# Adding the squared rows of two RMS norms on Pool, with one ones-matmul per tile in place of eight

## The reference

```
x = x + 1/2 * SwiGLU_1(RMSNorm(x))            # d_ff 2816
h = RMSNorm(x); z = h @ W_in                  # q 512 | k 128 | v 128 | u 512 | B 512 | C 512
attn = sliding-window (128) attention of 8 query heads on 2 key heads, with sinks and a relative bias
conv = B * causal_conv_width_3(C * u)
x = x + [RMSNorm(attn) | RMSNorm(conv)] @ W_out
x = x + 1/2 * SwiGLU_2(RMSNorm(x))
out = RMSNorm(x)

RMSNorm(x) = x * rsqrt(mean(x * x over the 1024 channels) + 1e-6) * g
```

## Time and profile before

| what | before |
|---|---|
| runs | 1294.57, 1296.29, 1334.91 us |
| median | 1296.29 us |
| span of the profiled execution, slowest core (core 6) | 1295.2 us |
| spans of the other cores | 1281.1 to 1292.5 us |
| PE busy | 1229.3 us (95%) |
| DVE busy | 462.7 us (36%) |
| ACT busy | 320.8 us (25%) |
| POOL busy | 169.5 us (13%), of it 167.0 in 316 weight loads |
| L349, ones-matmuls of these norms | 26.0 us busy, 380 ns each |

### The profile page before, as it was taken

How to read it: one execution, slowest core, us unless ns; L and a number is a source line. 1 busy time by engine, 2 the same in 40 slices (tenths; PEclk the granted TensorE clock), 3 DMA queues, 4 the chain that set the end, 5 groups by cost and what they waited for, 6 DMA issues and landing times.

```text
span 1295.2 us, 18401 instructions; the slowest of 8 cores (1281.1 to 1295.2 us)
## 1 busy us (share of the span) xinstructions
PE 1229.3 (95%) x6474; PEld 612.4 (47%) x6564; DVE 462.7 (36%) x791; ACT 320.8 (25%) x539; POOL 169.5 (13%) x324
## 2 busy tenths in 40 slices
PE   3899999999998999999999799999999999999996
PEld 1566656656554444444444344444444444444442
DVE  2623232253345523141273222313424552314125
ACT  3310101143444310101441001013344431010122
POOL 2011102102000121102111011110200012110200
PEclk9999999999998999999999989999999999999998
DMA  8653527417321873728429755362623146272713
GB/s 238 114 90 54 86 33 106 66 17 106 50 34 25 195 100 45 109 33 122 66 36 191 213 88 78 51 103 40 99 42 48 25 67 99 42 112 33 122 25 130
DMA packets 59352, 107.98 MB, mean 83 GB/s; under 512 B 5888, under 2 KB 11136, under 8 KB 59136
## 3 DMA queue, kind: packets, MB, share of 16 engines
q0 software_dynamic: 45504, 82.86, 42.5%
q1 hardware_dynamic: 12080, 20.71, 5.2%
q10 hardware_dynamic: 1680, 3.24, 0.8%
HBM read 181.24 MB, written 8.39 MB: 146 GB/s over the span
## 4 chain that ended last, share of the span: by engine, by line
PE 85%; DMA 8%; DVE 3%; ACT 2%; issue 2%; POOL 0%; SPq 0%; DVEq 0%; ACTq 0%; POOLq 0%
PE psall L485 43%; PE psall L546 23%; PE psall L574 8%; DMA outT<-xT_sb 4%; PE psall L840 4%; DMA ring_sb<-ws 2%; DMA xT_sb<-xT 2%; PE psall L349 2%; PE psall L490 1%; PE psall L734 1%; PE psall L733 1%; PE psall L663 1%; DVE xT_sb L415 1%; PE psall L610 1%; PE psall L729 1%
## 5 line engine op out<-in xcount | busy, mean ns | idle before, releaser
L485 PE MATMUL psall<-hT_sb,ring_sb 128*128 128x512 bf16 (+1 forms) x3055 | 616.1, 362 | 6.9 <-DMA ring_sb<-ws 4.0
L485 PEld LDWEIGHTS psall<-hT_sb,ring_sb 128*128 128x128 bf16 x3096 | 302.8, 98 | 317.2 <-issue 8.1
L546 PE MATMUL psall<-aT_sb,ring_sb 128*128 128x512 bf16 (+1 forms) x1561 | 320.3, 365 | 9.9 <-DVE xT_sb L553 8.6
L253 POOL DMA_DIRECT2D ring_sb<-ws x316 | 167.0, 538 | 1069.7 <-PE psall L485 413.0
L502 DVE TENSOR_TENSOR aT_sb<-psall,sS_sb 128x512 bf16<-128x512 f32 (+1 forms) x198 | 128.1, 647 | 463.4 <-PE psall L485 448.5
L500 ACT ACTIVATE sS_sb<-psall 128x512 f32<-128x512 f32 (+1 forms) x198 | 111.1, 561 | 704.9 <-PE psall L485 663.9
L546 PEld LDWEIGHTS psall<-aT_sb,ring_sb 128*128 128x128 bf16 x1584 | 155.6, 98 | 171.8 <-issue 16.3
L553 DVE SCALAR_TENSOR_TENSOR xT_sb<-psall,xT_sb 128x512 f32<-128x512 f32 (+1 forms) x216 | 139.7, 647 | 175.4 <-PE psall L546 162.0
L574 PE MATMUL psall<-hT_sb,ring_sb 128*128 128x384 bf16 (+3 forms) x675 | 126.4, 341 | 1.8 <-DVE rden_sb L759 0.8
L574 PEld LDWEIGHTS psall<-hT_sb,ring_sb 128*128 128x128 bf16 x680 | 66.4, 99 | 56.0 <-issue 6.1
L363 DVE SCALAR_TENSOR_TENSOR hT_sb<-xT_sb,gains_sb,psall 128x384 bf16<-128x384 f32 (+1 forms) x96 | 59.7, 675 | 33.0 <-ACT psall L354 30.1
(11 more groups left out here) (76 smaller groups left out, 375.9 us busy)
## 6 DMA issues: line engine op xcount, KB each, us to landing
ring_sb<-ws POOLq DMA_DIRECT2D x316, 256.0 KB, 5.4
outT<-xT_sb SPq DMA_DIRECT2D x6, 1024.0 KB, 17.2
xT_sb<-xT SPq DMA_DIRECT2D x2, 2048.0 KB, 18.5
xT_sb<-xT SPq DMA_DIRECT2D x2, 1536.0 KB, 31.1
convT_sb<-xT SPq DMA_DIRECT2D x1, 2048.0 KB, 12.7
outT<-xT_sb SPq DMA_DIRECT2D x4, 512.0 KB, 3.0
EB_sb<-biasT ACTq DMA_DIRECT2D x1, 1024.0 KB, 17.3
EB_sb<-xT SPq DMA_DIRECT2D x1, 1024.0 KB, 15.8
```

The costliest lines, as they stand in the source:

```text
L253: S.op("pool", lambda e, slot=slot, ci=ci: e.dma_start(out=ring[:, slot, :], in_=ws_d[ci]), writes=[("ring", slot)], dma=ringsem[slot], ex ...
L485: inst = e.matmul(ps[b][:, 0:n], lhsT=ring[:, s, kc * 128:(kc + 1) * 128], rhs=hT[:, kc, t0:t0 + n], start=(kc == 0), stop=(kc == 7))
L546: inst = e.matmul(ps[b][:, 0:n], lhsT=ring[:, s, o * 128:(o + 1) * 128], rhs=aT[:, fl, t0:t0 + n], start=(fl == 0), stop=(fl == len(dslots ...
```

## The change

`norm_sq_row` (the squares of the mixer's norm and of FFN2's norm, 9 tiles) is followed from the second row on by an add on Pool: rows 0 and 1, then the sum so far and the next row. The sum so far is f32 and lies in `anf[:, 0, :]`; the last add writes bf16 into the new `accb`. `norm_B0` then makes one ones-matmul on `accb` for such a tile. FFN1's first norm, the early norm of segment 1 and the final norm keep eight. The load into `anf` now waits for Pool's count at the end of the mixer too.

```
+        accb = sb("accb_sb", [128, 512], BF16)
+        accf = anf[:, 0, :]
...
+        summed = set()
+
+        def sum_rows(src, keys, n, o):
+            if o == 0:
+                return
+            first = src(0) if o == 1 else accf[:, 0:n]
+            dst, dk = (accb[:, 0:n], "accb") if o == 7 else (accf[:, 0:n], ("anf", 0))
+            rk = keys(o) + (keys(0) if o == 1 else [("anf", 0)])
+            S.op("pool", lambda e, o=o: e.tensor_tensor(out=dst, in0=first, in1=src(o), op=ALU.add), reads=rk, writes=[dk])
+
         def norm_sq_row(tile, o):
             t0, n = tile
             S.op("act", lambda e: e.activation(out=hT[:, o, t0:t0 + n], in_=xT[:, o, t0:t0 + n], func=AF.Square),
                  reads=blk_keys("xr", t0, n, o), writes=hkeys(t0, n, [o]))
+            sum_rows(lambda k: hT[:, k, t0:t0 + n], lambda k: hkeys(t0, n, [k]), n, o)
+            if o == 7:
+                summed.add(tile)
...
-            S.op("pe", mm, reads=hk + ["ones"], writes=[("ps", b)])
+            if tile in summed:
+                summed.discard(tile)
+                S.op("pe", lambda e: e.matmul(ps[b][:, 0:n], lhsT=ones[:], rhs=accb[:, 0:n], start=True, stop=True),
+                     reads=["accb", "ones"], writes=[("ps", b)])
+            else:
+                S.op("pe", mm, reads=hk + ["ones"], writes=[("ps", b)])
...
-            mixer_end.extend((...) for nm in ("pe", "act", "dve") if ...)
+            mixer_end.extend((...) for nm in ("pe", "act", "dve", "pool") if ...)
```

More of the change, by code:

```diff
@@ L899, in mixer @@
             del mixer_end[:]
-            mixer_end.extend((S.engs[nm]["sem"], S.engs[nm]["count"], nm) for nm in ("pe", "act", "dve") if S.engs[nm]["count"] > 0)
+            mixer_end.extend((S.engs[nm]["sem"], S.engs[nm]["count"], nm) for nm in ("pe", "act", "dve", "pool") if S.engs[nm]["count"] > 0)
         load_x_first(TILES_ALL[0][0])
```

## The result

The changed kernel took 1306.1 and 1306.5 us, against 1294.6 to 1296.3 us before. The ratio is 1.0082, with a 95% interval of 1.006 to 1.0103: 0.8% slower, clear of noise, and less than 2%. (Other executions of both kernels had a lower clock on part of the chip and took longer; all times and ratios here, and in the experiments, leave such executions out.) The forecast was 1302 us.

What follows compares the result with a forecast made beforehand. The slowest core and its TensorE chain were taken as the bound, at 1296 us. Gains of 4.4 us against losses of 10.7 (wait 5.3, clock 3.4, weight loads 1.0 and 1.0) gave +6, 1302 us; range 1290 to 1315.

Steps and rivals of the forecast that it cites:

- the clock: After PE's new idle stretch in the output projection the granted clock falls: 1.7 us twice, +3.4, range 0 to 6.8.
- What is removed: Seven fewer ones-matmuls at each of nine norm calls: 12.5 us of PE, the most the change can win.
- the wait at each call: At norm calls PE waits for Pool's last add, taken at 1.2 us (512 columns) or 0.9 (384).
- The gain at FFN2's last tiles: The call behind the gate projection, last tile of both segments, ends earlier: -1.3 us twice, -2.6.
- This place decides: FFN2's first tile, in the output projection: adds slower than half groups, PE idle 4.2 us; +2.6 twice, +5.3 us.
- The fourth q chunk: FFN1 to mixer, segment 0: weight loads begin 1.9 us later behind the last add, a stall of 1.0 us.
- The loads at FFN2's start: Eight weight loads move behind the last add and meet segment 0's x load: 1.0 us taken, up to 4.3.
- the add as quick as DVE's: Rival: Pool's add takes 0.7 to 0.8 us, the chain keeps up in the output projection; 1290 us, chance 0.16.
- the pitch above the row's: Rival: an add over 1.6 us, every call waits for the whole chain; 1338 us at 2.0, chance 0.06.
- a slow first add: Rival: Pool's first add, in FFN1, is late because its code must be fetched; 1306 us, chance 0.07.
- the third rival: Queue costs 4.3 us in segment 0, clock falls fully twice (6.8), add at 1.44 us; +18, 1314 us, chance 0.09.
- The sum: All places together: -4.4 us of gains and +10.7 of losses, about +6 us, 1302 us.

Runs made afterwards that it cites:

- Experiment 1: The changed kernel, but FFN2's norm keeps eight ones-matmuls for the first tile of each segment: ratio 1.0002 to the kernel before.
- experiment 2: The changed kernel, with the output projection's weight loads issued between the adds instead of all eight behind the last: ratio 1.0063 to the kernel before.
- experiment 3: The changed kernel, with segment 1's 4 MB x load held back until PE is at FFN2's last group: ratio 1.0061 to the kernel before.

## Why the prediction was right, point by point

The direction, the places and the chain of causes held. The size was 1302 us forecast against 1306.1 and 1306.5, because three terms were set too low: the clock and the two waits for weights.

- What is removed, and the wait at each call: held. The add was taken at 1.2 and 0.9 us and measured 1.155 and 0.913; the hand-over from one add to the next was taken at 0.1 and is 0.14. That the pitch of 1.3 is exact, and with it the 4.2 us of the next sentence, is luck: the two misses cancel. PE's wait in the output projection was forecast at 4.2 us and was 4.24, twice; in FFN1 at 1.2 and was 1.31 and 1.37 (384 columns). Over the eight calls 14.5 us. The gain at FFN2's last tiles was 1.1 us instead of 1.3 (from the gate product to the up product 3.45 us before, 2.36 after, in segment 0), since the last add there had to wait for the add before it. The estimate from the Trainium skill (GPSIMD Engine Reference, section 3.1), 1.12 us for 512 columns, is within 3% of the trace too. The same section of the Trainium skill has a rule to use DVE for elementwise work, which is not tested here: no run puts these adds on DVE.
- "This place decides": held. Experiment 1 undid those two calls alone and the time was that of before.
- The clock: the mechanism held, the term was too small. It took 1.7 us at each of two places; on core 7 it took 1.8 and 3.5 us, and 5.3 for the two together in the mean of the cores, against 3.4 forecast. The middle between "falls fully" and "doesn't fall" was taken from two cores after another wait, of 3.5 us; after 4.2 us it fell every time, if not for as long on every core.
- The fourth q chunk: 1.0 us forecast, 2.7 measured (1.3 to 2.8 by core). Two parts: the loads began 3.0 us after FFN1's end instead of 2.5, because the adds of the last rows queue behind one another when DVE is late, and the first load landed after 5.0 us instead of 3.7.
- The loads at FFN2's start: 1.0 forecast within bounds of 0 and 4.3; 4.1 on core 7 and 1.7 in the mean. The mechanism, a collision with the x load, is shown by experiments 2 and 3. The value was set near the lower bound, though the row of loads that run beside x transfers was at hand.
- Rivals: the add as quick as DVE's, the pitch above the row's, and a slow first add did not come. Of the third rival, the queue and the clock came near (4.1 of 4.3 us and 5.3 of 6.8, on core 7), the dearer add did not. The Trainium skill (GPSIMD Engine Reference, section 2.1) gives a delay of about 6 us before the first call of a freshly loaded kernel; the first Pool add here follows its square as closely as the others and took 0.91 us, so this add pays none that shows.
- The sum: +6 forecast, +10.6 by the ratio. With 5.3 for the clock, 2.7 and 4.1 for the two load waits it would have been +13 by core 7's numbers; this core's span rose by 14.9, the mean of the eight by 12.5.
- The base: the sum was added to the time of the slowest core, as if each core lost the same. Core 6 lost 2.5 us and another core became the slowest. The prediction had no term for that.

## What to carry to other kernels

Moving a reduction from a busy engine to an idle one pays only up to the last addend: what counts is the time from the last input to the result, not the work removed. Let the slower engine sum what is early and the faster one the last row or two; here that turned +0.8% into -0.7% with about three quarters of the adds kept. Before giving work to an engine that also issues loads, see what stands behind it in program order, and what other transfer starts at the moment to which those loads move.

## What the runs showed of the hardware

- Pool's two-input add: 1.155 us for 128x512 and 0.913 for 128x384, f32 or bf16 inputs and outputs alike. The difference is 1.89 ns a column, which leaves 0.19 us fixed, an estimate from these two widths. A step of a dependent chain costs 0.14 to 0.15 us more.
- TensorE at full work, then idle (one profiled execution for each length, two places on eight cores): after 1.7 us the granted clock stayed at 2.4 GHz in 16 of 16 cases, after 3.0 us it fell to 1.2 GHz for a while in 11 of 16, after 4.2 us in 16 of 16. Where it fell it cost some 1.6 to 3.5 us more. Before L663 the kernel before has a wait of 3.5 us, and there it fell on five of eight cores.
- A burst of eight weight loads that starts together with a 4 MB load of x: the third landed 14.1 us after issue (core 7), against 8.5 for the same burst without the x load (experiment 3, core 0). The x load itself took 21.8 us for its first part, against 11.6 in experiment 2, where the weight loads came earlier.
- Adds on Pool did not lengthen the instructions of DVE and ACT: the busy time of the two, on the slowest core, differs by 0.2 and 0.0 us between the two kernels.
